# A hybrid decoder layer in fp32: gate strips ahead of branch strips in a gated pass, and the delta-rule heads placed one behind another

## What is computed

```python
xn = rmsnorm(x, norm_mix)
xl, gl, q, k, v, z, b_raw, a_raw, u_pool, g_lru, g_dn, g_pool = split_cols(xn @ w_in)
h, h_last = rg_lru(causal_dwconv(xl), ...)           # width 1024
o_lru = h * gelu(gl)
o, s_last = gated_delta_rule(qh, kh, vh, beta, g, s0)  # 8 heads of 128 x 128, chunks of 128
o_dn = rmsnorm(o) * dn_norm_w * silu(z)
o_pool = multiscale_pool(u_pool, ...)
merged = (sigmoid(g_lru) * (o_lru @ w_br_lru) + sigmoid(g_dn) * (o_dn @ w_br_dn)
          + sigmoid(g_pool) * (o_pool @ w_br_pool))
x = x + merged @ w_out
hm = square(relu(rmsnorm(x, norm_mlp) @ w_up))
x = x + hm @ w_down
```

## Time and profile before

| | |
|---|---|
| time, median of 3 runs | 2197.82 us (2196.42 to 2201.01) |
| the profiled execution | 2197.58 us |
| its span, first to last instruction | 2195.8 us |
| mean granted clock of TensorE | 0.994 |
| PE busy | 2157.2 us (98%), 14507 products |
| VectorE (DVE) busy | 1223.4 us (56%) |
| ScalarE (ACT) busy | 784.4 us (36%) |
| GpSimd (POOL) busy | 176.0 us (8%) |
| HBM | 298.83 MB read, 8.37 MB written, 140 GB/s |

### The profile page before, as it was taken

How to read it: one execution, slowest core, us unless ns; L and a number is a source line. 1 busy time by engine, 2 the same in 40 slices (tenths; PEclk the granted TensorE clock), 3 DMA queues, 4 the chain that set the end, 5 groups by cost and what they waited for, 6 DMA issues and landing times.

```text
span 2195.8 us, 35754 instructions
## 1 busy us (share of the span) xinstructions
PE 2157.2 (98%) x14507; PEld 2096.5 (95%) x14507; DVE 1223.4 (56%) x1993; ACT 784.4 (36%) x946; POOL 176.0 (8%) x325
## 2 busy tenths in 40 slices
PE   8999998999999999999999999999999999999997
PEld 8998997899998899989999999999999999999997
DVE  7996786555566555555554554444444444444444
ACT  5434553222222222233333443333333333333243
POOL 7000011110022110010000100000000000000001
PEclk9999999999999999999999999999999999999998
DMA  6454444343354343346444444444444544444443
GB/s 216 140 158 135 130 126 132 107 121 113 96 171 125 107 122 109 96 136 197 149 146 153 151 143 149 150 153 146 152 148 150 153 146 149 153 148 153 145 144 106
DMA packets 295610, 308.96 MB, mean 141 GB/s; under 512 B 9713, under 2 KB 290417, under 8 KB 295233
## 3 DMA queue, kind: packets, MB, share of 16 engines
q1 hardware_dynamic: 291616, 291.54, 43.0%
q0 software_dynamic: 3584, 15.55, 2.4%
q10 hardware_dynamic: 288, 0.15, 0.0%
HBM read 298.83 MB, written 8.37 MB: 140 GB/s over the span
## 4 chain that ended last, share of the span: by engine, by line
PE 85%; DVE 8%; ACT 3%; issue 3%; POOL 1%; DMA 1%; DVEq 0%; ACTq 0%; SPq 0%; POOLq 0%
PE main L1420 26%; PE main L1421 25%; PE main L1422 25%; PE aux L1540 6%; DVE scratch L883 2%; DVE scratch L876 2%; DVE lo L876 1%; ACT hi L608 1%; DMA raw<-in_w_in 1%; DVE scratch L880 1%; PE aux L1523 0%; PE aux L1513 0%; POOL qkv L368 0%; DVE merged L876 0%; DVE scratch L879 0%
## 5 line engine op out<-in xcount | busy, mean ns | idle before, releaser
L876 DVE TENSOR_TENSOR lo<-raw,hi 128x1024 fp32r<-128x1024 f32 x546 | 670.0, 1235 | 571.6 <-ACT hi L608 565.4
L608 ACT ACTIVATE hi<-raw 128x1024 fp32r<-128x1024 f32 x546 | 573.4, 1056 | 934.8 <-PE main L1422 920.2
L1420 PE MATMUL main<-x_hi,hi 128*128 128x320 f32 x2688 | 842.8, 314 | 3.0 <-DVE x_lo L883 1.7
L1421 PE MATMUL main<-x_lo,hi 128*128 128x320 f32 x2688 | 831.6, 309 | 0.0
L1422 PE MATMUL main<-x_hi,lo 128*128 128x320 f32 x2688 | 831.5, 309 | 0.0
L1420 PEld LDWEIGHTS main<-x_hi,hi 128*128 128x128 f32 x2688 | 505.9, 188 | 10.5 <-issue 5.2
L1421 PEld LDWEIGHTS main<-x_lo,hi 128*128 128x128 f32 x2688 | 506.0, 188 | 0.8 <-issue 0.2
L1422 PEld LDWEIGHTS main<-x_hi,lo 128*128 128x128 f32 x2688 | 505.5, 188 | 0.0
L1420 PE MATMUL main<-o_hi,hi 128*128 128x320 f32 x1408 | 442.4, 314 | 4.6 <-DVE o_lo L876 4.6
L1421 PE MATMUL main<-o_lo,hi 128*128 128x320 f32 x1408 | 435.5, 309 | 0.0
L1422 PE MATMUL main<-o_hi,lo 128*128 128x320 f32 x1408 | 435.5, 309 | 0.0
(11 more groups left out here) (249 smaller groups left out, 1187.7 us busy)
## 6 DMA issues: line engine op xcount, KB each, us to landing
raw<-in_w_in SPq DMA_DIRECT2D x210, 512.0 KB, 3.7
raw<-in_w_up SPq DMA_DIRECT2D x128, 512.0 KB, 3.8
raw<-in_w_down SPq DMA_DIRECT2D x128, 512.0 KB, 3.4
raw<-in_w_back SPq DMA_DIRECT2D x80, 512.0 KB, 3.4
scratch<-in_s_in POOLq DMA_DIRECT2D x8, 512.0 KB, 4.7
out_s_out<-scratch POOLq DMA_DIRECT2D x8, 512.0 KB, 4.5
merged<-in_x SPq DMA_DIRECT2D x8, 320.0 KB, 7.7
qkv<-in_x POOLq DMA_DIRECT2D x1, 2560.0 KB, 10.4
```

The costliest lines, as they stand in the source:

```text
L608: act.activation(HI[:, slot * TILE:(slot + 1) * TILE], RAW[:, slot * TILE:(slot + 1) * TILE], ACT.Copy).then_inc(hi_ready, 1)
L876: return dve.tensor_tensor(out, a, b, op)
L1420: pe.matmul(bank, hi, xh, start=first, stop=False)
L1421: pe.matmul(bank, hi, xl, start=False, stop=False)
```

## The change

1. In a gated pass both gate strips come first (tiles 0 to 7), then both branch strips (8 to 11). There are two gate buffers, `GS` and a new `GS1`; `RN` and `BG`, which had space of their own, now lie in `GS`. VectorE's evacuations of gate strips stand at positions 8 and 12, the merges at 2 and 4 of what follows (before 8, 2 and 10, 4). SP's loads follow the new order. This holds for all three passes.
2. `gates(it)` of RG-LRU moves from behind tile 7 to behind tile 0 of the next iteration, for the last one behind tile 0 of the first gated pass.
3. The four heads of a half no longer stand one to an iteration: head i starts at 6.75 + 10.35 i tiles into the pass, with steps 1 and 2 at 0.8 and 2.1 tiles behind it and step k from 3 on at 2.6 + 0.5 (k - 3). There is no compressed first head. Rounded to eighths step 0 stands at (6, 5), (17, 0), (27, 3) and (37, 5), step 18 at (16, 6), (27, 1), (37, 3) and (47, 6).
4. The loops of RG-LRU on PE and of the first two gated passes on PE, ACT and VectorE are written out.

```diff
-        GS = sb("gate", 2 * N)
-        RN, BG = sb("qk_scale_rows", N), sb("beta_gamma_rows", N)
+        GS, GS1 = sb("gate", 2 * N), sb("gate_second", 2 * N)
+        GATE = (GS, GS1)
+        RN, BG = GS[:, 0:N], GS[:, N:2 * N]
...
                 for s in range(2):
                     for j in range(4):
-                        load(n0, 12, it, 6 * s + j, A["w_in"], j * 512, it * 512 + (G0[name] + s * 256))
+                        load(n0, 12, it, 4 * s + j, A["w_in"], j * 512, it * 512 + (G0[name] + s * 256))
+                for s in range(2):
                     for j in range(2):
-                        load(n0, 12, it, 6 * s + 4 + j, A["w_back"], BACK[name] + j * 512, it * 512 + s * 256)
+                        load(n0, 12, it, 8 + 2 * s + j, A["w_back"], BACK[name] + j * 512, it * 512 + s * 256)
 
...
-        def dn_place(k, peeled):
-
-
-            if peeled and k < 14:
-                return ((5, 3), (6, 1), (6, 4), (6, 6), (7, 0), (7, 2), (7, 4), (7, 6), (7, 7),
-                        (8, 1), (8, 2), (8, 4), (8, 6), (8, 7))[k]
-            if k < 6:
-                return ((1, 7), (2, 5), (3, 7), (4, 2), (4, 5), (4, 7))[k]
-            return (5 + (k - 6) // 2, (3, 7)[k % 2]) if k < 18 else (11, 6)
-
-        def dn_steps(step, h, peeled, late):
+        def dn_place(i, k):
+
+            at = 6.75 + 10.35 * i + (0.0, 0.8, 2.1)[k] if k < 3 else 6.75 + 10.35 * i + 2.6 + 0.5 * (k - 3)
+            eighth = int(round(8 * at))
+            return (eighth - 1) // 8, (eighth - 1) % 8
+
+        def dn_steps(step, h0, it):
 
             steps = {}
-            for k in range(19):
-                pos = dn_place(k, peeled)[0] + 4
-                if (pos > 12) == late:
-                    steps.setdefault(pos - 12 * late, []).append(lambda k=k: step(h, k))
+            for i in range(4):
+                for k in range(19):
+                    at = dn_place(i, k)[0] + 4 - 12 * it
+                    if 0 < at <= 12:
+                        steps.setdefault(at, []).append(lambda i=i, k=k: step(h0 + i, k))
             return steps
...
             def gate(n0, t0, it, s):
-                tile_done(n0, 12, it, 6 * s + 3)
-                dve.wait_ge(evacuated, it * 8 + (t0 + 4 * s + RING))
-                for m in range(2):
-                    tt(GS[:, m * N:(m + 1) * N], MB[m][:, 0:N], R[:], ALU.mult).then_inc(evacuated, 1)
+                tile_done(n0, 12, it, 4 * s + 3)
+                dve.wait_ge(evacuated, it * 8 + (t0 + 2 * s + RING))
+                for m in range(2):
+                    tt(GATE[s][:, m * N:(m + 1) * N], MB[2 * s + m][:, 0:N], R[:], ALU.mult).then_inc(evacuated, 1)
 
             def merge(n0, t0, g0, it, s, branch):
 
-                tile_done(n0, 12, it, 6 * s + 5)
+                tile_done(n0, 12, it, 2 * s + 9)
                 dve.wait_ge(gate_ready, it * 2 + (g0 + s + 1))
                 for m in range(2):
-                    dst = GS[:, m * N:(m + 1) * N] if branch else cols(MG, it, 4 * N, (2 * s + m) * N, N)
-                    stt(dst, GS[:, m * N:(m + 1) * N], 1.0, MB[2 + m][:, 0:N], ALU.add, ALU.mult) \
+                    own = GATE[s][:, m * N:(m + 1) * N]
+                    dst = own if branch else cols(MG, it, 4 * N, (2 * s + m) * N, N)
+                    stt(dst, own, 1.0, MB[2 * s + m][:, 0:N], ALU.add, ALU.mult) \
                         .then_inc(evacuated, 1)
                 if not branch:
                     return
-                dve.wait_ge(evacuated, it * 8 + (t0 + 4 * s + 4 + RING))
+                dve.wait_ge(evacuated, it * 8 + (t0 + 2 * s + 6 + RING))
                 sums = cols(MG, it, 4 * N, 2 * s * N, 2 * N)
-                ins = tt(sums, sums, GS[:], ALU.add)
+                ins = tt(sums, sums, GATE[s][:], ALU.add)
...
-            def gated(it, n0, t0, g0, h0, branch, after, peeled=False):
-                own = {8: [lambda: gate(n0, t0, it, 0)], 10: [lambda: merge(n0, t0, g0, it, 0, branch)]}
+            def gated(it, n0, t0, g0, h0, branch, after):
+                own = {8: [lambda: gate(n0, t0, it, 0)], 12: [lambda: gate(n0, t0, it, 1)]}
                 if h0 is not None:
-                    own = joined(own, dn_steps(dn_step, it + h0, peeled, False))
+                    own = joined(own, dn_steps(dn_step, h0, it))
                 walk(split, n0, 12, it, 12, joined(after, own))
             def late(it, n0, t0, g0, h0, branch):
-                steps = {2: [lambda: gate(n0, t0, it, 1)], 4: [lambda: merge(n0, t0, g0, it, 1, branch)]}
-                return steps if h0 is None else joined(steps, dn_steps(dn_step, it + h0, False, True))
-
-            gated(0, GPL_N, GPL_T, 0, 0, 0, lru_steps(lru_step, 3), True)
-            with dve.Fori(1, 4) as it:
-                ch.enter(it, 1, LINKS["gpl"])
+                steps = {2: [lambda: merge(n0, t0, g0, it, 0, branch)], 4: [lambda: merge(n0, t0, g0, it, 1, branch)]}
+                return joined(steps, dn_steps(dn_step, h0, 4)) if h0 is not None and it == 3 else steps
+
+            gated(0, GPL_N, GPL_T, 0, 0, 0, lru_steps(lru_step, 3))
+            for it in range(1, 4):
                 gated(it, GPL_N, GPL_T, 0, 0, 0, late(it - 1, GPL_N, GPL_T, 0, 0, 0))
-                ch.leave(3, "gpl")
...
-                    3: [(7, lambda: qk_sums(3))], 7: [(7, lambda: gates(0))]})
-            with pe.Fori(1, 4) as it:
-                lru(it, {7: [(7, lambda: gates(it))]})
+                    3: [(7, lambda: qk_sums(3))]})
+            for it in range(1, 4):
+                lru(it, {0: [(7, lambda it=it: gates(it - 1))]})
...
-            def gated(it, n0, t0, h0, first, o0, between=None):
+            def gated(it, n0, t0, h0, first, o0, between=None, dn_first=None):
                 between = dict(between or {})
                 if h0 is not None:
-                    for k in range(19):
-                        j, b = dn_place(k, first is not None)
-                        between[j] = list(between.get(j, ())) + [(b, lambda k=k: dn_step(it + h0, k, first))]
+                    for i in range(4):
+                        for k in range(19):
+                            j, b = dn_place(i, k)
+                            if it * 12 <= j < it * 12 + 12:
+                                between[j - 12 * it] = list(between.get(j - 12 * it, ())) + [
+                                    (b, lambda i=i, k=k: dn_step(h0 + i, k, dn_first if i == 0 else None))]
                 for s in range(2):
-                    strip(n0, 12, t0, 8, it, 6 * s, 4 * s, XH, XL, between=between)
-
-                    strip(n0, 12, t0, 8, it, 6 * s + 4, 4 * s + 2, OH, OL,
+                    strip(n0, 12, t0, 8, it, 4 * s, 2 * s, XH, XL, between=between)
+                for s in range(2):
+                    strip(n0, 12, t0, 8, it, 2 * s + 8, 2 * s + 4, OH, OL,
                           waits=(lambda i: (o_ready, o0 + 2 * (i + 1))) if first is not None and s == 0 else None,
                           tiles=2, between=between)
 
-            gated(0, GPL_N, GPL_T, 0, 4, 0)
-            with pe.Fori(1, 4) as it:
+            gated(0, GPL_N, GPL_T, 0, 4, 0, {0: [(7, lambda: gates(3))]}, dn_first=4)
+            for it in range(1, 4):
                 gated(it, GPL_N, GPL_T, 0, None, 0)
```

More of the change, by code:

```diff
@@ L1651, in _ @@
                                15: [(7, lambda: pool_product(2))]})
-            gated(0, GPP_N, GPP_T, 4, 8, 4, {3: [(7, lambda: pool_product(3))]})
-            with pe.Fori(1, 4) as it:
+            gated(0, GPP_N, GPP_T, 4, 8, 4, {3: [(7, lambda: pool_product(3))]}, dn_first=8)
+            for it in range(1, 4):
                 gated(it, GPP_N, GPP_T, 4, None, 4)
```

46 lines of the change are left out of this document (19 added, 27 removed).

## The result

| | before | after |
|---|---|---|
| time, median (range, runs) | 2198.44 us (2196.42 to 2201.01, 4) | 2231.27 us (2229.8 to 2233.48, 4) |
| span of the profiled execution | 2195.8 us | 2229.1 us |
| mean granted clock | 0.994 | 0.987 |

The changed kernel takes 1.0152 times as long, 95% interval 1.0135 to 1.0168: slower by 33 us. The forecast was 2221.5 with a range of 2206 to 2234: the time measured is inside it, 9.8 us above the forecast.

The account below looks back on a forecast made before the run. PE, busy for 98% of the span, was taken as the bound. Terms 1.5 - 2.2 - 19.5 + 13.5 + 13.3 + 6.2 + 1.5 + 7.2 + 2.5 = +24.0 on 2197.58 gave 2221.5 us, range 2206 to 2234.

Parts of the forecast that it names:

- RG-LRU's gate products, +1.5: RG-LRU: convolution wait goes but moves to tile 4; iterations 2 and 3 gain nothing, iteration 1 gets the delay, +1.5 us.
- Entry: Start of first pass: o_lo wait goes, about 4 us of wait stands before the first head's broadcast; -2.2 us.
- Waits gone from the earlier trace: Heads: waits of steps 2 to 5 and compressed heads go, with the half clock after L1566; -19.5 us.
- `dn_done`, 13.5: Between heads: step 0 waits for VectorE's updates of S after step 18, 2.25 us six times; +13.5 us.
- Step 18, 6.2: Heads 0, 3 and others: step 17 is ready after step 18 is due, 3.1 us a half; +6.2 us.
- POOL's chain to step 3, 13.3: Between heads: store, reload and mask delay step 1's products and step 3, waits of 2.9, 2.1, 1.65 us; +13.3 us.
- Half clock, 2.5: Slow clock after the 4 us wait and one or two step-3 waits; +2.5 us.
- Gate and merge collisions, 7.2: Both passes: other gate evacuations and merges meet head steps, 1.65 us in the first, 5.55 in the second; +7.2 us.
- Rival A: Between heads: PE need not stop, updates of S and reload lie beside its tiles; 2194.7 us, chance 0.08.
- Rival B: RG-LRU: its waits go for good because the chain has unseen slack, 10 us less; 2211.5 us, chance 0.07.
- Rival C: Between heads: the reload is not that late, 1.1 us less in six transitions; 2215 us, chance 0.08.
- Rival D: All eight waits of 2 us and more bring 3.41 us at half clock, 1.1 us more each; 2230 us, chance 0.10.

Follow-up runs that it names:

- the square: Four kernels crossing gate products (behind tile 7 or next tile 0) with heads' places (before or change), ratios to before: 0.9994, 1.0095, 1.0055, 1.0152.
- experiment 1: The changed kernel with VectorE subtracting the next iteration's tile 0 before RG-LRU's convolution, not behind it: 2222.37 us, ratio 1.0111.
- Experiment 2: The changed kernel with RG-LRU's gate products back behind tile 7: 2219.82 us, ratio 1.0095.
- experiment 4: The changed kernel with POOL masking the decay before it waits for the previous head's stores and reloads: 2231.45 us, ratio 1.0144.
- Experiment 7: The changed kernel with steps 0 and 1 of every head later and POOL's masks ahead of its wait for the stores: 2223.99 us, ratio 1.0116.
- experiment 5: The changed kernel with the heads' places of the kernel before; gates first and the later gate products stay: 2209.45 us, ratio 1.0055.
- experiment 8: The changed kernel with the old heads' places and the gate products back behind tile 7, so gates first alone: 2196.79 us, ratio 0.9994.
- experiment 6: The changed kernel with steps 0 and 1 of every head put off to 0.6 and 1.2 tiles: 2229.28 us, ratio 1.0138.
- experiment 9: The changed kernel with gate products behind tile 7, mask before the store wait, first head from 7.25, heads every 10.4 tiles, steps every 0.45: 2221.47 us, ratio 1.0107.

## Why the prediction was right, and where not

The direction was right, the time lies in the range, and the two passes became as much longer as forecast. The time is 9.8 us over the forecast (2231.3 for 2221.5), nearly all of it in RG-LRU. In the passes the sum is right and its composition is not, and that is luck. By its steps:

- **RG-LRU's gate products, +1.5: the term that was mis-sized.** It cost 12.5 to 13.5 us (the square), 8.9 of them in iterations 1 to 3 of RG-LRU (104.58 us for 95.69). The step that failed is "behind the next tile 0 that wait goes". The wait at tile 4 for the GL banks came as forecast (4.2 us, 4 times). But the convolution stands between tile 7 and the subtraction of tile 0 on VectorE, and the eight products behind tile 7 had been PE's work while that subtraction ran. Taken away, they left PE waiting at tile 0, some 9 us (10.4 in the first row of the waits, 1.6 in experiment 1), and 3.41 us at half clock; experiments 1 and 2 take that back, by 8.9 and 11.5 us. The products were followed on every engine, the queue of the tile put ahead of them was not.
- **The heads' places and the entry of the pass**, all other terms, summed to +22.5; the square has 21 to 22. Nearly all of the forecast's part is waiting: the clock is in it with 2.5 us less the 2.3 counted as won. Experiment 2 has 9.8 us of idle time and 12.1 of longer busy time. By parts:
  - Entry: 4 us of wait forecast, 3.7 measured.
  - Waits gone from the earlier trace rows: L1566's 5.0 us went, with the half clock behind them. Of the later steps' 3.6 and 2.1 us nothing can be booked as won, since rows of 2.7 and 5.4 us stand in their place.
  - `dn_done`, 13.5: all six, 10.3 us idle; the rows give 0.16 more each. Four are 1.99 us. The two behind a late step 18 are 1.2, because at half clock the two blocks ahead of the broadcast cover more of the same wait.
  - Step 18, 6.2: 4.4 us idle, 1.50 at heads 0 and 4 where 1.8 was said, 0.70 at heads 3 and 7.
  - **POOL's chain to step 3, 13.3, did not come out**: L1177 waited 2.7 us in all, and experiment 4 took the mask out of the chain without an effect that can be told. Two steps of the forecast failed here. It took 5.0 us for POOL's wait for the stores, from the kernel before; in four of the six transitions it was about 3, and in two of these, at full clock, the mask was in time and step 3 idled 0 and 0.31 us. In the other two, heads 0 to 1 and 4 to 5, the reload was as late as forecast, but PE was late too, at half clock, and step 3 idled 0.61 and 1.34 us for 2.9.
  - **Half clock, 2.5**: 34 us more of it in the passes. Its price is not measured by itself. PE's busy time there rose by 9.5 and 4.8 us (269.62 for 260.14, 266.19 for 261.35) with the same work but for eight products (about 1 us), so by 13 us that need an explanation. Experiment 7 has only 6.9 us more half clock than before and is still 6.4 us up, by the same count. The 27.3 us of half clock between the two thus brought 6.9 us, which would make it 9 us for the 34. An estimate from these rows: 9 to 13 us, where 2.5 was written; what the rest is, no run shows. The 1.15 us taken for each 3.41 us was low: products of 320 columns start 0.267 us apart there (438.60 to 439.93 in the change) and 0.147 at full clock, 1.5 us lost in 3.41.
  - Gate and merge collisions, 7.2, and step 3 of head 0, 1.5: not tested alone. The row of L1528 for VectorE's operations, 2.1 us in the earlier trace rows, is 5.4 now. Experiments 5 and 8 show that what they cost belongs to the places, not to gates first.
  - So one term of 13.3 us that did not come was made up for by a clock term that was some 7 to 10 us too small. The text had the clock "under POOL's chain"; in two transitions it is the other way round, and in two others there was no half clock and no late reload.
- **Rival A** (no stop between heads): refuted by the six waits. But experiments 6 and 9, which take them away, gained 2 us and nothing, as other steps then stood too close.
- **Rival B** (the RG-LRU waits go for good): wrong, they grew.
- **Rival C** (an earlier reload): its mechanism came in four of six transitions. The reload went out 4.4 us after POOL issued the first store at heads 1 to 2, 6.5 at heads 0 to 1; the store itself landed in a median 4.2 us for 4.5 before. That is why the forecast's chain is missing where the clock was full. The estimate of 3.2 us from the Trainium skill's "DMA: Bandwidth & Descriptors", "Anatomy of one DMA", is still 1.0 us under that 4.2.
- **Rival D** (slow clock behind the waits, 2230) names a mechanism that the passes show, at nearly the time measured; but part of that time is RG-LRU's. By the rule on HAM oscillation of the Trainium skill's "TensorE: Matmul & The Clock Gate", a PE that waits in every round pays in every round; the trace agrees in four of six transitions.
- **Rival E**: the order was as the table says.
- The sign "passes 10 and 13 us longer" measured 13.3 and 13.1; "step 1's products idle 2 us for the mask" did not show, and "step 3 idles 1 to 2.7" was 1.3 at most.

What stays open: how the 21 to 22 us of the places split between step 18's wait, `dn_done` and the clock. Each experiment that took one away gave it to another, and none took away step 18's wait alone.

## What to carry to other kernels

When a piece of PE's work is moved past a point where PE waits, ask what that piece covered there: the tile behind it comes due earlier, and its operands may stand in another engine's queue behind the very work that is waited for. A chain of dependent steps packed to its own length has no slack to move: distance given to one pair of steps is taken from another, and only a run of the whole shows it. Before a chain is priced as a wait, see whether the engine that would wait is itself on time, and whether a store or load in the chain takes the same time in all its places.

## What the runs showed of the hardware

Of the same wait at the same place in three iterations (2.4 us at tile 0), one was followed by half clock, for 3.41 us:

```profile
266.74:270.15 3.41, 3.41 (x15) 3.41 (x14) 1.31 (x2) 0.00 (x0) 0.00 (x0) 0.50 0.86 258
```

and two by none. Between heads the clock did not fall behind `dn_done` alone. In the first and third of the four windows (427.17 and 768.50) it had already fallen 6.7 and 5.8 us before the broadcast, 1.5 and 1.9 us after step 18's wait of 1.50 us. That wait of heads 0 and 4 was followed by half clock both times here, and in experiments 1, 2, 4 and 6, which have it too; in experiment 7 once of two. The `dn_done` waits of 1.99 us met a fall of the clock in two of four places here (498.85 and 901.62), and in three of four in experiments 1, 2 and 4. What else decides it no run shows.

Where the clock fell between heads it stayed low for 6.83 to 13.65 us, though PE was busy for 88% or more of each of these windows. That a wait under 2 us can cost more in clock than in waiting was not expected: 1.50 us at step 18 of head 0 stood at the head of 13.65 us at half speed.
